# A two-block transformer on one NeuronCore: the first normalisation by column quarters, and four smaller moves in the first layer

## The chip, the core and the metric

The kernel is one program on one core of a Trainium2 chip. The metric is the device time of one launch in microseconds (us), median of the runs. The engines are TensorE (PE; its weight loads are listed as PEld), VectorE (DVE), ScalarE (ACT), GpSimd (POOL) and SyncE (SP), which here issues nearly all large DMAs. Each runs its own instructions in order, and they meet through semaphores.

## What is computed

A sequence of 256 tokens with model width 2048 goes through two layers of a first block (latent attention beside a gated convolution) and one layer of a second block. Only the first layer of the first block, and what feeds it, is touched:

```python
for l in range(2):
    mod = silu(c) @ ada_w[l] + ada_b[l]               # [2048] @ [2048, 6144]
    shift, scale, gate = split(mod, 3)
    h = rms_norm(x, norm_g[l]) * (1 + scale) + shift
    z = h @ w_in[l]
    q_lat, kv_lat, k_rope, mla_gate, conv_in, conv_gate = split(z)   # 512, 256, 64, 1024, 2048, 1024 columns
    q = rms_norm(q_lat) @ w_q_up[l];  kv = rms_norm(kv_lat) @ w_kv_up[l]
    # rms_norm and rotation of q and k, causal attention, times silu(mla_gate)
    u = (u_val + b) * sigmoid(u_gate + b)             # conv_in split in two
    u = silu(layer_norm(depthwise_conv31(u)))         # mean and variance over 1024 channels
    conv_out = (u @ w_pw[l] + b_pw[l]) * silu(conv_gate)
    x = x + gate * (concat(mla_out, conv_out) @ w_out[l])
```

## The kernel before

**Products.** Every large matrix product is a `Product`: blocks of 256 output columns, each of units of 4 row tiles (a unit of weights is 128 x 1024 floats, 0.5 MB). The activations are kept as `h_hi` + `h_lo` and each weight unit as `w_hi` (ACT rounds it) + `w_lo` (DVE subtracts, or POOL for the products `gate` and `cgate`), and PE adds three products per tile (L1705). A product with `lo=None` is native: no split, PE reads `w_raw`. There are 8 slots for raw units (`RAW`) and 4 for split ones (`PARTS`). SP, ACT, DVE and PE each walk the same list of products, written by hand in the order lat, krope, ua, ub, gate, cgate, kv, q, pw, outca, outcb, outm for a layer; `ahead` lets each engine prepare the next block beside the present one, and `beside` hooks put other work between units.

**The modulation vector.** `silu(c) @ ada_w` is made by loading `ada_w` in pieces of 128 x 1024 floats (0.5 MB) and adding each, scaled by a column of `c_act`, into an accumulator on DVE (L1137, in the first two groups L1156). A group of 32 pieces gives 2048 numbers; PE then sums it over the partitions (`reduce_mod`, L1729) and DVE adds the bias (`mod_out`, L1145). Groups 0 (shift) and 1 (scale) of layer 0 are loaded first of all through 8 slots; group 2 (gate) is spread by `ada=(...)` beside lat, krope and ua, group 3 beside ub, q and pw, group 4 beside outca and outcb. SP issues a piece right behind the weight unit it stands beside, and waits first for its slot of 4 (`ASLOTS`) to be consumed on DVE.

**The start.** SP loads the 64 pieces of groups 0 and 1 (L584), DVE adds them, PE transposes x, the small parameters and the convolution's taps (L1823, L1832, L1839), and sums the squares of x (L1737). After `mod_out(1)` DVE splits four weight units and makes the 16 tiles of h (L1216, L1221), and only then PE starts `lat`. After krope PE sums the squares of the latents (L1743).

**The convolution.** From the end of `ub`, DVE runs the 31 taps in four channel pairs (L1370, L1374), 2 steps beside each unit of `gate` and 6 beside each of `cgate`. Since POOL splits the weights of these two products, nothing else holds DVE there. `mod_out(2)` stands on DVE between the two products, `reduce_mod(2)` on PE ahead of `gate`. PE sums the conv output for the mean after units 2, 8 and 13 of `cgate` (`MEAN_STEPS`, L1872) and after unit 1 of `q` (`LAST_MEAN_STEP`), and its squares for the variance after unit 3 of `q` (`VAR_STEP`, L1718). Each sum waits for its pair's last tap. DVE subtracts the mean (L1389), ACT squares (L919), and after the variance DVE and ACT finish what `pw` reads.

## Time and profile before

| | us |
|---|---|
| median of 3 runs | 2280.22 (2279.74 to 2280.77) |
| profiled execution | 2277.91 |
| its span | 2276.1 |
| PE busy in it | 2148.8 (94%) |
| DVE busy in it | 1704.7 (75%) |
| ACT busy in it | 964.9 (42%) |

The page gives the busy time of each engine, 40 slices of the span, the chain that ended last and groups by line. The profiled execution is 1.8 us longer than its span and 2.3 us below the median. Matmuls overlap, so a row's duration is not its pace: the pace is the time from start to start.

### The profile page before, as it was taken

How to read it: one execution, taken by the hardware profiler on the slowest of the kernel's cores; microseconds unless marked ns; L12 is line 12 of the kernel's file. 1: busy time of each engine (PE TensorE's matmuls, PEld its weight loads, DVE VectorE, ACT ScalarE, POOL GpSimd, SP SyncE). 2: the span in 40 equal slices, each digit the busy share in tenths (PEclk: the TensorE clock that was granted, in tenths of full speed). 3: DMA queues.
4: the chain of work that ended last, by engine and by line, in shares of the span. 5: the costliest groups of instructions: out<-in, count | busy, mean ns of one | idle time of the engine just before them, and what ended most of it. 6: DMA issues, size and time to landing. Idle time of an engine off the chain costs nothing.

```text
span 2276.1 us, 39704 instructions
## 1 busy us (share of the span) xinstructions
PE 2148.8 (94%) x15541; PEld 2037.9 (90%) x15541; DVE 1704.7 (75%) x2347; ACT 964.9 (42%) x1512; POOL 214.3 (9%) x130
## 2 busy tenths in 40 slices
PE   2289999999999999999999999999999999999997
PEld 2289997889999978899999999999999999988886
DVE  6988997697999976877875887788876565653554
ACT  2144445325534353354454445455544444444443
POOL 0000481000006700033000000000000000000000
PEclk7599999999999999999999999999999999999999
DMA  9989965896898577969946996568866555566663
GB/s 329 351 286 360 300 175 192 275 324 222 296 373 256 149 268 252 316 177 293 364 135 224 375 372 199 173 201 272 275 207 207 180 181 184 184 214 186 191 193 122
DMA packets 390357, 559.41 MB, mean 246 GB/s; under 512 B 25544, under 2 KB 316944, under 8 KB 389725
## 3 DMA queue, kind: packets, MB, share of 16 engines
q1 hardware_dynamic: 386304, 550.70, 73.6%
q0 software_dynamic: 1456, 4.28, 0.8%
q10 hardware_dynamic: 2476, 2.82, 0.4%
q8 instruction: 76, 1.25, 0.2%
q14 instruction: 45, 0.36, 0.0%
HBM read 555.57 MB, written 2.18 MB: 245 GB/s over the span
## 4 chain that ended last, share of the span: by engine, by line
PE 85%; DVE 6%; ACT 3%; issue 3%; DMA 3%; SPq 0%; ACTq 0%; DVEq 0%
PE gemm L1705 80%; DMA ada_first<-in_ada_w 2%; DVE w_lo L1169 2%; DVE ada_even L1137 1%; PE stat L1729 1%; ACT w_hi L784 1%; DVE ada_acc L1156 0%; DVE scr L1216 0%; DVE ada_odd L1137 0%; PE bankT L1810 0%; DMA w_raw<-in_w_out 0%; PE gemm L1799 0%; PE bankO L1799 0%; PE stat L1872 0%; DVE h_lo L1221 0%
## 5 line engine op out<-in xcount | busy, mean ns | idle before, releaser
L1705 PE MATMUL gemm<-h_hi,w_hi 128*128 128x256 f32 (+1 forms) x3312 | 945.0, 285 | 17.6 <-DVE h_lo L1221 12.6
L1169 DVE TENSOR_TENSOR w_lo<-w_raw,w_hi 128x1024 fp32r<-128x1024 f32 x540 | 654.3, 1225 | 386.3 <-ACT w_hi L784 385.0
L1705 PE MATMUL gemm<-h_lo,w_hi 128*128 128x256 f32 (+1 forms) x3312 | 939.0, 284 | 0.0
L1705 PE MATMUL gemm<-h_hi,w_lo 128*128 128x256 f32 (+1 forms) x3312 | 939.0, 284 | 0.0
L784 ACT ACTIVATE w_hi<-w_raw 128x1024 fp32r<-128x1024 f32 (+1 forms) x604 | 619.7, 1041 | 694.6 <-PE gemm L1705 554.8
L1705 PEld LDWEIGHTS gemm<-h_hi,w_hi 128*128 128x128 f32 (+1 forms) x3312 | 634.5, 192 | 21.2 <-issue 15.9
L1705 PEld LDWEIGHTS gemm<-h_lo,w_hi 128*128 128x128 f32 (+1 forms) x3312 | 634.6, 192 | 0.6
L1705 PEld LDWEIGHTS gemm<-h_hi,w_lo 128*128 128x128 f32 (+1 forms) x3312 | 634.3, 192 | 0.3
L1137 DVE SCALAR_TENSOR_TENSOR ada_even<-ada_raw,c_act,ada_even 128x1024 f32<-128x1024 f32 x160 | 210.5, 1316 | 4.9 <-DMA ada_raw<-in_w_ada 1.7
L658 POOL TENSOR_TENSOR w_lo<-w_raw,w_hi 128x1024 fp32r<-128x1024 f32 x64 | 160.9, 2518 | 413.5 <-ACT w_hi L784 413.2
L1137 DVE SCALAR_TENSOR_TENSOR ada_odd<-ada_raw,c_act,ada_odd 128x1024 f32<-128x1024 f32 x128 | 169.5, 1325 | 5.3 <-DMA ada_raw<-in_ada_w 1.8
L1705 PE MATMUL gemm<-w_hi,G_hi 128*128 128x512 f32 x352 | 137.9, 392 | 1.8 <-DVE G_lo L1630 1.8
L1705 PE MATMUL gemm<-w_lo,G_hi 128*128 128x512 f32 x352 | 137.1, 389 | 0.0
L1705 PE MATMUL gemm<-w_hi,G_lo 128*128 128x512 f32 x352 | 137.0, 389 | 0.0
L1705 PE MATMUL gemm<-mixsrc,w_raw 128*128 128x256 f32 x512 | 115.3, 380 | 1.6 <-ACT krT L771 1.6
L1705 PEld LDWEIGHTS gemm<-mixsrc,w_raw 128*128 128x128 f32 x512 | 95.6, 190 | 14.2 <-ACT krT L771 2.2
L1374 DVE SCALAR_TENSOR_TENSOR bankT<-u_pad,dwT,bankT 128x256 f32<-128x256 f32 x232 | 91.2, 480 | 0.1
L1374 DVE SCALAR_TENSOR_TENSOR bankS<-u_pad,dwT,bankS 128x256 f32<-128x256 f32 x232 | 91.2, 480 | 0.0
L1705 PEld LDWEIGHTS gemm<-w_hi,G_hi 128*128 128x128 f32 x352 | 66.1, 188 | 15.3 <-DVE G_lo L1630 2.0
L1705 PEld LDWEIGHTS gemm<-w_lo,G_hi 128*128 128x128 f32 x352 | 66.1, 188 | 14.0
L1705 PEld LDWEIGHTS gemm<-w_hi,G_lo 128*128 128x128 f32 x352 | 66.1, 188 | 13.5
L1705 PE MATMUL gemm<-m_hi,w_hi 128*128 128x256 f32 x256 | 73.2, 286 | 2.5 <-DVE m_lo L1261 2.5
(350 smaller groups left out, 2661.1 us busy)
## 6 DMA issues: line engine op xcount, KB each, us to landing
w_raw<-in_w_in SPq DMA_DIRECT2D x264, 512.0 KB, 6.0
w_raw<-in_w_up SPq DMA_DIRECT2D x176, 512.0 KB, 3.5
ada_raw<-in_ada_w SPq DMA_DIRECT2D x160, 512.0 KB, 7.0
ada_raw<-in_w_ada SPq DMA_DIRECT2D x160, 512.0 KB, 6.4
w_raw<-in_w_out SPq DMA_DIRECT2D x96, 512.0 KB, 6.3
w_raw<-in_w_down SPq DMA_DIRECT2D x88, 512.0 KB, 3.7
ada_first<-in_ada_w SPq DMA_DIRECT2D x32, 512.0 KB, 8.8
ada_late<-in_w_ada SPq DMA_DIRECT2D x32, 512.0 KB, 5.2
```

The lines of the kernel that those rows point to most:

```text
L658: pool.tensor_tensor(w_lo[:, fixed % PARTS, 0:sz], w_raw[:, fixed % RAW, 0:sz], w_hi[:, fixed % PARTS, 0:sz].bitcast(F32), ALU.subtract).t ...
L784: act.activation(w_hi[:, fixed % PARTS, 0:sz], w_raw[:, fixed % RAW, 0:sz], ACT.Copy).then_inc(w_hi_done, 1)
L1137: dve.scalar_tensor_tensor(out=acc, in0=(ada_late if n == 11 else ada_raw)[:, slot, :], scalar=c_act[:, 0 if n < 6 else 1, bass.ds(m, 1)], ...
L1169: dve.tensor_tensor(w_lo[:, fixed % PARTS, 0:sz], w_raw[:, fixed % RAW, 0:sz], w_hi[:, fixed % PARTS, 0:sz].bitcast(F32), ALU.subtract).th ...
L1374: ins = dve.scalar_tensor_tensor(out=conv[:, ch, :] if k == TAPS - 1 else acc, in0=src, scalar=w, in1=acc, op0=ALU.mult, op1=ALU.add)
L1705: last = pe.matmul(half(g, k, q), left, right, start=(kt == 0 and j == 0 and (q == 0 or g.wide)), stop=(u == len(g.units) - 1 and t == nk ...
L1729: last = pe.matmul(stat[:, CB2 * t:CB2 * t + P], acc[:, j * AC + t * P:j * AC + (t + 1) * P], ones_and_halves[:, CB2:], start=(j == 0), st ...
```

## The change

**Start.** `FSLOTS` is 10, and groups 0 and 1 are loaded by column quarters: one piece now holds one row of every 16 of the matrix (`(k j)`, j = 16), and of it 512 columns of each of the two groups, so packets of 2 KB where they had 4 KB. Of the 16 pieces of a quarter, PE takes four itself (`BY_PE`, eight matmuls each with the piece as weights and `c16`, 16 columns, moving) and DVE adds the other twelve; `first_reduce` adds DVE's part in the same bank. `first_tiles` then makes 4 tiles of h. The products lat and krope of layer 0 become one product `first` of 4 blocks, which keeps all four in the `gemm` banks and adds 4 row tiles per quarter. SP loads its weights after the tenth piece of each quarter. The rope angles, the transposes of parameters and taps, and the small DMAs of ACT are spread over the quarters.

**Group 2** of layer 0 is added beside ua and ub (16 pieces each); `reduce_mod(2)` goes behind `gate` on PE in layer 0, while `mod_out(2)` keeps its place on DVE. **Groups 3 and 4** of layer 0 are placed by the table `SPREAD`. **The mean's last sum** goes to kv's unit 6, the **variance** to q's unit 1. **k's scaling** moves from DVE to ACT. **The latent sums** are made in two halves after units 4 and 5 of ua, in both layers, and their root and rows after units 8 and 13. ua and outm run as one body without a loop.

```diff
-FSLOTS = 8
+FSLOTS = 10
+W_AHEAD = 10
+ROPE_STEP = 5
+FROUNDS = -(-2 * AU // FSLOTS)
...
-LAST_MEAN_STEP = 1
-VAR_STEP = 3
+LAST_MEAN_STEP = 6
+VAR_STEP = 1
+LATENT_STEP, ROOT_STEP, ROWS_AT = 4, 8, 13
...
+QUARTERS = 4
+KQ = KT // QUARTERS
+FROWS = DM // P
+FCOLS = AC // 2
+BY_PE = (0, 1, 7, 11)
+PAR_EARLY = 10
+PAR_SPLIT = 24
+SUM_COLS = 16
+SPREAD = {"kv": [1] * 6 + [0] * 2, "q": [1] * 4 + [2] * 4, "pw": [1, 1, 1, 0] * 2, "outca": [2] * 8, "outcb": [2] * 8,
+          "outm": [0, 1] * 8}
 MOD_STEP = 1
 UP_FIRST = 8
...
+            if l == 0:
+                first = G["first"] = product("first", wi, QUARTERS, CB, full, QUARTERS, "a", h_hi, h_lo, plain(0))
...
+        pieces = [(n, j) for n in (3, 4) for j in range(AU)]
+        for name, counts in SPREAD.items():
+            g = G[name, 0]
+            g.ada, g.plan = None, []
+            for c in counts:
+                g.plan.append(pieces[:c])
+                pieces = pieces[c:]
...
+            def ada_load_first(qt, j):
+                m = FROWS * qt + j
+                slot = m % FSLOTS
+                if m >= FSLOTS:
+                    if by_pe(m - FSLOTS):
+                        sp.wait_ge(first_by_pe, pieces_up_to(m - FSLOTS, True))
+                    else:
+                        sp.wait_ge(ada_used, pieces_up_to(m - FSLOTS, False))
+                src = a["ada_w"][0][:, 0:2 * GROUP].rearrange("(k j) (g n) -> k j g n", j=FROWS, g=2)[
+                    :, j, :, FCOLS * qt:FCOLS * (qt + 1)]
+                sp.dma_start(first_slot(slot)[:, 0, :].rearrange("p (g n) -> p g n", g=2), src).then_inc(ada_loaded[slot], 16)
+            def load_first(qt):
+                for b, (k0, nk) in enumerate([(KQ * qt, KQ)] * 4):
+                    n, fixed = first.unit(0, qt, b)
+                    if fixed >= RAW:
+                        sp.wait_ge(w_used, n - RAW + 1)
+                    c, cols = first_cols(b)
+                    src = first.weights.rearrange("(k p) n -> p k n", p=P)[:, k0:k0 + nk, c:c + cols]
+                    dst = w_raw[:, fixed % RAW, 0:nk * cols].rearrange("p (k n) -> p k n", k=nk)
+                    sp.dma_start(dst, src).then_inc(w_loaded[fixed % RAW], 16)
...
+            for qt in range(QUARTERS):
+                for j in range(FROWS):
+                    if j == W_AHEAD:
+                        load_first(qt)
+                    ada_load_first(qt, j)
+            load(G["ua", 0], 0, 0)
...
+            def late_consts(part):
+                for x in (par_dmas[PAR_EARLY:PAR_SPLIT], par_dmas[PAR_SPLIT:])[part]:
+                    par_load(*x, const_loaded)
+                if part == 0:
+                    return
+                for l in range(LAYERS):
+                    act.dma_start(dw_rows[:, l, :], a["dw_w"][l]).then_inc(const_loaded, 16)
+                    for s, v in enumerate((a["q_norm_g"], a["k_norm_g"])):
...
+                act.wait_ge(k_inverse, l + 1)
+                act.wait_ge(k_rope_out, l + 1)
+                for t in range(TT):
+                    for h in range(NH):
+                        ins = act.activation(k_tok[:, t, h, :], k_tok[:, t, h, :], ACT.Copy,
+                                             scale=ss[:, 0, t * NH + h:t * NH + h + 1])
...
-                    link(dve.reciprocal(ss[:, 0, :], ss[:, 0, :]))
-                    dve.wait_ge(k_rope_out, l + 1)
-                    for t in range(TT):
-                        for h in range(NH):
-                            ins = dve.tensor_scalar(k_tok[:, t, h, :], k_tok[:, t, h, :],
-                                                    ss[:, 0, t * NH + h:t * NH + h + 1], None, ALU.mult)
-                    ins.then_inc(qk_ready, 1)
+                    dve.reciprocal(ss[:, 0, :], ss[:, 0, :]).then_inc(k_inverse, 1)
...
+            def first_tiles(qt):
+                first_low(qt, 0)
+                first_low(qt, 1)
+                cols = slice(KQ * qt, KQ * (qt + 1))
+                sums_ = first_sums(qt)[:, 0:2 * KQ * SUM_COLS].rearrange("p (g t c) -> p g t c", g=2, c=SUM_COLS)[:, :, :, 0]
+                bias_ = par[:, 0:2 * KT].rearrange("p (g t) -> p g t", g=2)[:, :, cols]
+                done, count = (first_taken, qt // 2 + 1) if qt % 2 == 0 else (stat_read, USE[f"first{qt}"] + 1)
+                if qt % 2 == 0:
+                    dve.wait_ge(first_summed, qt // 2 + 1)
+                else:
+                    stat_wait(dve, f"first{qt}")
+                dve.tensor_tensor(mod[:, 0:2, cols], sums_, bias_, ALU.add).then_inc(done, 1)
+                dve.wait_ge(done, count)
+                link(dve.scalar_tensor_tensor(out=gainA[:, cols], in0=mod[:, 1, cols], scalar=1.0,
+                                              in1=par[:, 3 * KT + KQ * qt:3 * KT + KQ * (qt + 1)], op0=ALU.add, op1=ALU.mult))
+                for t in range(KQ * qt, KQ * (qt + 1) + 2):
+                    if t < KQ * (qt + 1):
+                        dve.scalar_tensor_tensor(out=scr[:, t, :], in0=xT[:, t, :], scalar=gainA[:, t:t + 1],
+                                                 in1=rstd[:, 0, :], op0=ALU.mult, op1=ALU.mult).then_inc(t_ready, 1)
+                    if t >= KQ * qt + 2:
+                        c = t - 2
+                        dve.wait_ge(h_hi_ready, c + 1)
+                        dve.scalar_tensor_tensor(out=h_lo[:, c, :], in0=scr[:, c, :], scalar=mod[:, 0, c:c + 1],
+                                                 in1=h_hi[:, c, :].bitcast(F32), op0=ALU.add,
+                                                 op1=ALU.subtract).then_inc(h_ready, 1)
+                first_low(qt, 2)
+                first_low(qt, 3)
...
+            def first_piece(qt, j):
+                m = FROWS * qt + j
+                slot = m % FSLOTS
+                if j == BY_PE[0]:
+                    if qt % 2:
+                        stat_write(pe, f"first{qt}")
+                    elif qt:
+                        pe.wait_ge(first_taken, qt // 2)
+                pe.wait_ge(ada_loaded[slot], 16 * (m // FSLOTS + 1))
+                for t in range(2 * KQ):
+                    last = pe.matmul(first_sums(qt)[:, t * SUM_COLS:(t + 1) * SUM_COLS],
+                                     first_slot(slot)[:, 0, t * P:(t + 1) * P], c16[:, j, :],
+                                     start=(j == BY_PE[0] and t == 0), stop=False, skip_group_check=True)
+                last.then_inc(first_by_pe, 1)
...
+            def first_reduce(qt):
+                pe.wait_ge(ada_used, pieces_up_to(FROWS * (qt + 1) - 1, False) if qt < QUARTERS - 1 else 2 * AU)
+                for t in range(2 * KQ):
+                    last = pe.matmul(first_sums(qt)[:, t * SUM_COLS:(t + 1) * SUM_COLS],
+                                     first_acc[:, qt % 2, t * P:(t + 1) * P], ones[:, 0:SUM_COLS],
+                                     start=False, stop=(t == 2 * KQ - 1), skip_group_check=True)
+                last.then_inc((first_summed, stat_ready)[qt % 2], 1)
...
+            for qt in range(QUARTERS):
+                more = BY_PE if qt + 1 < QUARTERS else ()
+                for j in more[0:2]:
+                    first_piece(qt + 1, j)
+                first_unit(qt, 0)
+                first_unit(qt, 1)
+                for j in more[2:3]:
+                    first_piece(qt + 1, j)
+                first_unit(qt, 2)
+                first_unit(qt, 3)
+                for j in more[3:]:
+                    first_piece(qt + 1, j)
+                if qt == 1:
+                    par_turned()
+                if more:
+                    first_reduce(qt + 1)
             pe.wait_ge(halves_done, 1)
-            reduce_mod(0)
...
+                def latent_sums(_, n, l=l):
+                    if n == LATENT_STEP:
+                        pe.wait_ge(lat_squared, l + 1)
+                        stat_write(pe, f"lat{l}")
+                    if n in (LATENT_STEP, LATENT_STEP + 1):
+                        for j in range(3 * (n - LATENT_STEP), 3 * (n - LATENT_STEP) + 3):
+                            last = token_sums(0 if j < 4 else TT, lat_sq[:, j, :], j == 0, j in (3, 5))
+                        if n == LATENT_STEP + 1:
+                            last.then_inc(stat_ready, 1)
+                    if n == ROWS_AT:
+                        inverse_rows(f"lat{l}", 2)
...
-                reduce_mod(3 * l + 2)
+                if l:
+                    reduce_mod(3 * l + 2)
                 multiply(G["gate", l])
+                if not l:
+                    reduce_mod(3 * l + 2)
...
-                multiply(G["kv", l])
+                multiply(G["kv", l], lambda _, n: mean(CT // 2 - 1) if n == LAST_MEAN_STEP else None)
                 def variance(_, n):
-                    if n == LAST_MEAN_STEP:```

What stands in a row on each engine at three places. First DVE between `ub` and the mean's subtraction in layer 0 (bankS and bankT hold the taps' running sums; L1370/L1591 open a pair). Before:

```order
L1370 TENSOR_SCALAR bankT<-u_pad,dwT,par 128x256 x2
L1145 TENSOR_TENSOR mod<-stat,par 128x16
L1374 SCALAR_TENSOR_TENSOR bankT<-u_pad,dwT,bankT 128x256 x58
L1374 SCALAR_TENSOR_TENSOR conv<-u_pad,dwT,bankT 128x256 x2
L1370 TENSOR_SCALAR bankS<-u_pad,dwT,par 128x256 x2
```

and, after the change, from the same read of `stat` on:

```order
L1309 TENSOR_TENSOR mod<-stat,par 128x16
L1595 SCALAR_TENSOR_TENSOR bankT<-u_pad,dwT,bankT 128x256 x58
L1595 SCALAR_TENSOR_TENSOR conv<-u_pad,dwT,bankT 128x256 x2
L1591 TENSOR_SCALAR bankS<-u_pad,dwT,par 128x256 x2
L1595 SCALAR_TENSOR_TENSOR bankS<-u_pad,dwT,bankS 128x256 x58
L1595 SCALAR_TENSOR_TENSOR conv<-u_pad,dwT,bankS 128x256 x2
L1591 TENSOR_SCALAR bankT<-u_pad,dwT,par 128x256 x2
L1595 SCALAR_TENSOR_TENSOR bankT<-u_pad,dwT,bankT 128x256 x58
L1595 SCALAR_TENSOR_TENSOR conv<-u_pad,dwT,bankT 128x256 x2
L1293 MEMSET ada_odd 128x1024
L1301 SCALAR_TENSOR_TENSOR ada_odd<-ada_raw,c_act,ada_odd 128x1024 x6
L1610 SCALAR_TENSOR_TENSOR conv<-stat,conv 128x2048
```

The read of `stat` stands in the same place, inside the second pair, but what fills `stat` now comes behind `gate` on PE; and a memset and six pieces stand between the last tap and the mean's subtraction.

Second, SP's queue at `kv` (the weights of kv, two blocks, then a piece behind each block), after the change:

```order
L691 DMA w_raw<-in_w_in 128x4x256 x28
L691 DMA w_raw<-in_w_kv_up 128x2x256 x2
L678 DMA ada_raw<-in_ada_w 128x1x1024
L691 DMA w_raw<-in_w_kv_up 128x2x256
L678 DMA ada_raw<-in_ada_w 128x1x1024
L691 DMA w_raw<-in_w_kv_up 128x2x256
L678 DMA ada_raw<-in_ada_w 128x1x1024
```

Before, no piece stood beside kv. Third, DVE at the start of the third quarter after the change (c_102 is `c16`):

```order
L1335 TENSOR_TENSOR w_lo<-w_raw,w_hi 128x1024 x2
L1350 TENSOR_TENSOR mod<-bankO,par 128x2x4
L1352 SCALAR_TENSOR_TENSOR gainA<-mod,par 128x4
L1356 SCALAR_TENSOR_TENSOR scr<-xT,gainA,rstd 128x256 x3
L1361 SCALAR_TENSOR_TENSOR h_lo<-scr,mod,h_hi 128x256
L1356 SCALAR_TENSOR_TENSOR scr<-xT,gainA,rstd 128x256
L1361 SCALAR_TENSOR_TENSOR h_lo<-scr,mod,h_hi 128x256 x3
L1335 TENSOR_TENSOR w_lo<-w_raw,w_hi 128x1024
L1335 TENSOR_TENSOR w_lo<-w_raw,w_hi 128x256
```

Before, one such stretch of 16 tiles stood behind all 64 pieces.

## Rows read from the trace of the kernel before

**Rows 1.** The page: busy time of each engine.

```profile
PE 2148.8 (94%) x15541; PEld 2037.9 (90%) x15541; DVE 1704.7 (75%) x2347; ACT 964.9 (42%) x1512; POOL 214.3 (9%) x130
```

**Rows 2.** Waits of PE: what, for what, us in total, times, longest.

```profile
PE stat L1729 <- DVE mod L1145: 39.3, 1, 39.3
PE bankS L1823 <- ACT xT L771: 19.7, 1, 19.7
```

**Rows 3.** Chain that ended last, 60 to 170 us: start, us, what.

```profile
109.29 1.28 DVE ada_acc L1156
110.81 5.19 PE stat L1729 x32
...
116.30 4.63 DVE w_lo L1169 x4
121.05 1.28 DVE scr L1216 x3
...
122.87 42.20 PE gemm L1705 x336
165.07 2.57 PE stat L1743 x24
```

**Rows 4.** Windows: PE, PEld, DVE, ACT, POOL busy; clock, DMA share, GB/s.

```profile
8.00:36.00 28.00, 2.79 (x12) 2.42 (x12) 18.21 (x15) 0.00 (x0) 0.00 (x0) 0.74 1.03 395
...
140.00:164.00 24.00, 24.00 (x204) 24.00 (x203) 20.09 (x21) 9.86 (x15) 0.00 (x0) 1.00 1.05 358
168.00:172.00 4.00, 4.00 (x23) 4.00 (x23) 4.00 (x4) 3.91 (x7) 0.00 (x0) 0.57 1.08 376
...
386.00:426.00 40.00, 39.24 (x165) 30.92 (x165) 32.26 (x49) 15.30 (x52) 0.00 (x0) 1.00 1.04 364
```

**Rows 5.** The same of PE alone: PE busy, clock, DMA share, GB/s.

```profile
124.00:128.00 4.00, 4.00 (x23) 0.58 0.14 52
```

**Rows 6.** Timeline of PE in the start: start, us, line, operation.

```profile
59.28 7.03 PE L1839 MATMUL bankT<-ident,dw_rows 31*128 31x31 f32 x32
```

**Rows 7.** Critical chain, 255 to 400 us, in layer 0 from ub's end on.

```profile
262.73 1.79 PE stat L1729 x16
264.52 54.71 PE gemm L1705 x456
...
353.50 24.73 PE gemm L1705 x128
...
379.12 2.30 DVE conv L1389
...
381.45 1.91 ACT ln_sq L919
...
387.98 10.59 PE gemm L1705 x32
...
399.05 1.10 PE gemm L1705 x4
```

**Rows 8.** Timeline of DVE in the convolution and behind it.

```profile
292.34 0.17 DVE L1145 TENSOR_TENSOR mod<-stat,par 128x16 f32<-128x16 f32 x1
...
340.46 0.98 DVE L1370 TENSOR_SCALAR bankT<-u_pad,dwT,par 128x256 f32<-128x256 f32 x2
...
364.08 0.86 DVE L1374 SCALAR_TENSOR_TENSOR conv<-u_pad,dwT,bankT 128x256 f32<-128x256 f32 x2
...
400.27 3.76 DVE L1422 TENSOR_SCALAR k_tok<-k_tok,ss 128x192 f32<-128x192 f32 x16
```

**Rows 9.** Timeline of PE at kv's end and in q.

```profile
359.09 19.13 PE L1705 MATMUL gemm<-w_raw,lat 128*128 128x256 f32 x80
...
378.92 5.32 PE L1705 MATMUL gemm<-w_raw,lat 128*128 128x384 f32 x16
384.08 3.62 PE L1718 MATMUL stat<-ln_sq,ones_and_halves 128*128 128x256 f32 x16
```

**Rows 10.** Issues of DMA by line: KB each, median us to landing.

```profile
w_raw<-in_w_kv_up SPq DMA_DIRECT2D x16, 256.0 KB, 2.8
```

410 lines of the change are left out of this document (268 added, 142 removed).

## Prediction

> **What bounds the kernel now.** I read the page first: PE is busy for 2148.8 of 2276.1 us [rows 1], so 127 us are left. The waits of PE name two long ones, both ahead of the first large product: 39.3 us for the second modulation vector and 19.7 us for the copy of x [rows 2]. Behind the start, only PE's own work, or a wait that is put in its way, can move the end. The chain then dates the start: DVE ends the last of 64 pieces at 110.6, PE sums them to 116.0, four weight units are split to 120.9, PE begins at 122.87 and ends lat and krope at 165.07 [rows 3]. In that stretch DMA is the supplier: 395 GB/s with 4 KB packets alone, and 358 GB/s where 1 KB weight packets are mixed in [rows 4]. Last I read layer 0 from 262 to 400 on both engines, since the diff moves a sum there. On PE one product follows the other [rows 7, 9]. DVE ends the taps at 364.9 [rows 8], 13 us ahead of the sum behind the kv row (359.09 + 19.13 = 378.2) that needs the last of them [rows 9].
>
> **Start.** Behind 165.07 the same products follow as now, so the gain is 165.07 less the time at which PE ends `first`.
>
> Bytes ahead of it: 64 pieces of 0.524 MB are 33.5, the latent weights 2048 x 832 x 4 B are 6.8, x is 2.1, small ones 0.5: 43 MB. At 395 GB/s for all that is 109 us, at 358 it is 120 us [rows 4]. Packets of 2 KB lie between the two kinds that the rows show, so I take 115, plus 2 for the beginning. DVE's work in a quarter is 12 pieces of 1.28, three and a quarter splits of 1.2 and eight tile operations of 0.43 [rows 3]: 23 us, against 27 to 29 us of DMA, so it follows. But at each border DVE frees no slot for some 8 us, and I add 4 us in all. The last piece lands at 121.
>
> Behind it: DVE adds it (1.3), PE sums (16 records, at 5.19/32 = 0.16 each: 2.6), bias and gain 0.4, three scr and one h_lo 1.7 [rows 3]. Then 84 matmuls. At the low level, 1.2 GHz, 256 columns take 0.213; at the high one the row of 456 shows 0.12 [rows 7]. The first 24 low are 5.1 and 60 high 7.2. The splits lie beside PE's sum. Together 18.3, so `first` ends at 139 to 140. I take 140: **25 us gained**. Bounds: all bytes at 395 and no loss at the borders, 132 (33 gained); all at 358 and 8 us lost there, 150 (15 gained).
>
> PE's added work is 16 pieces of 16 records (2.6 each). It is hidden as long as PE's quarter is shorter than that of DMA: 10.4 + 2.6 + 84 matmuls (10.1 to 17.9) = 23 to 31 us, against 27 to 29. The taps' transposes (7.0 [rows 6]) stand in the second quarter, in what PE has left; if they had no cover, they would cost 7 there.
>
> **Latent sums.** They are loads of weights with one column moving. Behind the 24 of them in layer 0 the clock is granted at 0.57, which is mostly the 1.2 GHz level, from 168 to 172, and 23 matmuls fit in 4 us where 4/0.12 = 33 would [rows 4]: 10 x 0.12 = 1.2 us, and some ahead of it. In two halves between units PE's dense work resumes sooner. I take **1.5 us gained**, bounds 0 and 3 (both layers).
>
> **Late gate sum.** On PE it costs 1.79 in either place. But DVE reads it and stays where it was. In the times of the trace before, DVE reaches that read at 292.3 and finds it done [rows 8]. Now PE does gate first: 384 matmuls of 0.12 from 262.7 end at 308.8, the sum at 310.6 [rows 7]. DVE waits from 292.3 to 310.8, **18.3 us**, with all later taps queued behind, since it is in order. A pair takes 24.4 (340.5 to 364.9), so pairs 1 to 3 end at 334.4, 358.8 and 383.2 instead of 316.1, 340.5 and 364.9 [rows 8].
>
> PE asks for pair 2 at 352.6 (0.87 ahead of the 353.50 row [rows 7]) and gets it at 358.8: **6.2 us lost**; the sum ends at 359.7, two units of cgate (5.8) at 365.5. The kv row of 19.13 holds 80 records, 64 of kv and 16 of q; two units of q are 5.32, so a kv unit is 13.8/8 = 1.7 [rows 9]. Six of them end at 375.8.
>
> **Pieces by plan.** The fifth piece beside kv needs the slot of the first, which DVE adds behind the last tap: 383.2 + memset 0.9 (an estimate) + 1.3 = 385.4. Behind that piece in SP's queue stand the weights of kv's block 6. They go out at 386.2 and land after 2.8 [rows 10] plus 1.4 for the piece ahead: 390.4. So PE waits there **14.6 us**, and this covers the wait for the last tap. Block 6 ends at 392.1, the mean's last sum at 393.0.
>
> **Mean and variance sooner.** DVE has by then added its six pieces (384.1 + 7.7 = 391.8), subtracts in 2.3: 395.3; ACT squares in 1.9: 397.3 [rows 7]. PE does the last kv unit and two of q (1.7 + 5.3) to 400.0: no wait. Variance 3.6, six units of q at 2.65 15.9 [rows 9]: 419.5. What pw reads is ready before: it took 11.4 us from the variance's end at 387.7 [rows 9] to 399.05 [rows 7], and PE has 15.9 of q here. So pw starts at 419.5 against 399.05: **20.4 us lost** in layer 0. Of that the wait of 0.48 ahead of pw goes in both layers (387.98 + 10.59 = 398.57 [rows 7]): 1 us gained. Bounds of the loss: 22 at the top; 13 if SP's queue does not bind and only the taps do (6.2, then 383.2 - 377.4 = 5.8 at the mean, and 1 at the variance).
>
> **The rest at nothing.** k's scaling, 3.8 us on DVE [rows 8], becomes 16 ACT instructions. ACT is busy for 15.3 of the 40 us there [rows 4]; without that cover PE would wait up to 8 (16 of 0.5) ahead of the transposes. Eight pieces moved into outm: DVE has a block of 5.8 us of PE's and needs 2.4 + 1.3 + 1.2 = 4.9; uncovered they would be 10. Beside ua and ub each unit still has one piece, 1.05 MB in 2.88 us. Layer 1 keeps its sum ahead of gate, so it has no such stall. Bounds 0 to 4 lost.
>
> **Sum.** Span: -25 - 1.5 + 20.4 - 1 = -7.1. Profiled execution 2277.9 - 7.1 = 2270.8; the median stood 2.3 above it: **2273 us**.
>
> **Two rules of the Trainium skill.** The page "DMA: Bandwidth & Descriptors" (Bandwidth) gives about 358 GB/s as a core's share of HBM when both cores of a pair stream. The trace shows 395 with one core running [rows 4]. By that rule the 43 MB would take 120 us and the total would be 5 us more.
>
> "TensorE: Matmul & The Clock Gate" (HAM oscillation) says that an array which waits for data between bursts drops to its slow clock and begins every burst there. The trace agrees for the first burst: 0.58 from 124 to 128 [rows 5]. What that would do to the quarters is rival 2.
>
> **Rivals.**
> 1. *DVE's wait costs PE next to nothing* (the convolution catches up, or the read comes later than I think). For it: 13 us of lead. Against: the wait is 18.3, and a later pair has 24.4 us on DVE against at most 18.1 between two sums on PE. Then the start counts, and 1.5 us at kv's block 6 (365.8 + 1.3 + 0.8 + 4.2 = 372 against 369.5 to 370.5 for PE): -25 - 1.5 - 1 + 1.5 = -26: 2254. Chance 0.17.
> 2. *PE bounds the quarters at the low clock* (the other side). The place is each quarter; the price is its 84 matmuls at 0.213 instead of 0.12. Then a quarter is 31 us, the first sum comes at 44, and with the taps (7) `first` ends at 44 + 3 x 31 + 7 + 21 = 165: nothing gained, and with 20.4 lost the time is 2298. The sign turns against the change by more than 4.6 us when `first` ends behind 152. For it: 0.58 in the first burst [rows 5]. Against: dense matmuls follow each other for 10 us and more in each quarter, and 23 in those 4 us are already more than the 19 of an all-low stretch. Chance 0.08.
> 3. *The parameters land late* and hold PE in its second quarter, and with it the slots. The copies of x waited 19.7 us for ACT [rows 2], which issues these DMAs. A hold of 8 us beyond the slack: 2281. Chance 0.12.
> 4. *The start streams at 395 GB/s*: `first` ends at 133, 2266. Chance 0.13.
>
> The forecast has 0.50.
>
> **How the numbers follow.** A measurement of this kernel can tell 0.2%, 4.6 us, from no change. Faster by more is below 2275.7: rivals 1 and 4, and 0.40 of the forecast's 0.50: 0.70. Within it: 0.10 of the forecast and most of rival 3: 0.21. Slower: rival 2 and the rest: 0.09. The range goes from rival 1 (2253) to where rival 2 decides (2284).
>
> **What would show it.** In the profile after: `first` ends near 140; DVE waits some 18 us for the sum of group 2, at about 266; PE waits near 326 for the conv output and near 349 for kv's weights; pw starts near 393, although ua starts 25 us earlier; the clock is full behind the latent sums. If DVE's wait is there and PE's are not, rival 1 holds. If `first` ends behind 150 with PE busy at a low clock, rival 2.

## The result and the profile after

The changed kernel takes 2290.13 us (median of 5, 2288.06 to 2291.11), the kernel before 2279.92 on the same chip: a ratio of 1.0038 (95% interval 1.0027 to 1.005). It is 10.2 us slower, where the forecast was 7 faster, and the time lies outside the range. The profiled execution took 2289.61 with a span of 2287.8, 11.7 above the 2276.1 of before.

PE's busy time went up by 52 us [rows 1]; that alone says nothing yet, since most of it is the start, where PE used to wait:

```profile
PE 2201.2 (96%) x15798; PEld 2089.3 (91%) x15798; DVE 1673.0 (73%) x2302; ACT 976.3 (43%) x1543; POOL 214.1 (9%) x130
```

PE's waits (what, for what, us in total, times, longest). The two of [rows 2] are gone. The first and the last row are new and lie in layer 0, the other two are the new start:

```profile
PE gemm L1920 <- DMA w_raw<-in_w_kv_up: 12.3, 1, 12.3
PE stat L2072 <- DVE first_acc L1324: 9.1, 1, 9.1
PE bankO L2045 <- DMA ada_raw<-in_ada_w: 8.8, 1, 8.8
PE stat L2172 <- DVE conv L1595: 6.3, 1, 6.3
```

The chain that ended last, in the start (start, us, what), which answers to [rows 3]:

```profile
36.15 8.80 PE stat L1952 x32
...
59.59 15.78 DMA ada_raw<-in_ada_w
...
76.74 3.60 PE stat L2072 x16
80.34 6.83 PE bankO L2045 x32
87.17 7.54 PE gemm L2090 x48
94.70 1.69 PE bankO L2045 x16
...
103.26 5.93 PE bankT L2110 x32
109.19 3.53 PE bankO L2072 x16
112.72 6.83 PE stat L2045 x32
...
135.54 1.80 PE stat L2072 x16
...
139.59 12.81 PE gemm L2090 x84
```

L2045 is a piece that PE adds, L2072 the sum that closes a quarter, L2090 `first`, L2110 the taps' transposes. Read it backwards: `first` ends at 139.59 + 12.81 = **152.40**, not at 140. The last link is as long as I said (16.9 us from 135.54 on, against 18.3 less the 1.3 of DVE's last piece). But the last sum begins at 135.5, where I had the last piece landed at 121. From 76.74 to 135.54 the chain is PE alone, but for 0.4 us of a copy on ACT at 102.8: 58.8 us for two quarters. And 76.74 is late already: it hangs on a transfer of 15.8 us, which SP could issue only when DVE had freed its slot at 59.6.

Windows of the start (PE, PEld, DVE, ACT, POOL busy; clock, DMA share, GB/s), answering to [rows 4]:

```profile
30.00:45.00 15.00, 12.44 (x51) 11.10 (x52) 6.42 (x5) 0.39 (x2) 0.00 (x0) 0.68 1.05 382
45.00:60.00 15.00, 13.55 (x98) 13.47 (x97) 14.00 (x22) 5.41 (x9) 0.00 (x0) 0.77 1.07 358
60.00:75.00 15.00, 7.69 (x67) 7.59 (x67) 11.04 (x18) 3.49 (x4) 0.00 (x0) 0.85 0.85 289
75.00:90.00 15.00, 13.26 (x62) 13.26 (x63) 12.80 (x19) 3.50 (x7) 0.00 (x0) 0.50 0.92 292
105.00:120.00 15.00, 15.00 (x71) 14.94 (x72) 9.04 (x16) 5.54 (x9) 0.00 (x0) 0.50 1.03 351
```

My 115 us were 43 MB at 374 GB/s. From 30 to 60 us the rows come near that (382, 358), from 60 to 90 they show 290. SP's own waits say what it lacked: slots. Of its first 140 us it waited 21.2 for pieces that DVE adds (the first row and 2.9 more in another) and 16.6 for pieces that PE adds (the second row and 5.8 more); from 55 to 80 us it was 15.4, all for DVE's:

```profile
SPq L661 <- DVE first_acc L1324: 18.3, 19, 3.7
SPq L661 <- PE bankO L2045: 10.8, 4, 4.1
```

The kernel before had such dips too, with rows of 4 KB, which [rows 4] leave out (columns as above):

```profile
40.00:50.00 10.00, 8.87 (x41) 7.51 (x40) 5.32 (x5) 8.09 (x20) 0.00 (x0) 0.90 0.82 272
60.00:70.00 10.00, 10.00 (x50) 9.94 (x50) 9.54 (x19) 2.27 (x4) 0.00 (x0) 0.54 1.00 377
70.00:80.00 10.00, 1.52 (x14) 1.33 (x12) 9.55 (x8) 0.00 (x0) 0.00 (x0) 0.81 0.54 175
```

From 105 to 120 PE is busy for all of it at a clock of 0.50 in the changed kernel: there the 16 records of a piece take 3.4 us (6.83/2), at the full clock 1.69.

Layer 0, timelines of DVE and of PE (in brackets the wait ahead and what ended it), answering to [rows 7 to 9]:

```profile
297.05 0.17 DVE L1309 TENSOR_TENSOR mod<-stat,par 128x16 f32<-128x16 f32 x1 [18.17 <-PE stat L1944]
```

```profile
345.31 2.07 PE L2172 MATMUL stat<-conv,ones_and_halves 128*128 128x256 f32 x4 [6.26 <-DVE conv L1595]
377.15 3.75 PE L1920 MATMUL gemm<-w_raw,lat 128*128 128x256 f32 x8 [12.35 <-DMA w_raw<-in_w_kv_up]
...
407.52 7.72 PE L1920 MATMUL gemm<-conv,w_raw 128*128 128x256 f32 x35
```

DVE waits 18.2 for the sum of group 2 (forecast 18.3), PE 6.3 for the second pair (6.2) and 12.3 for kv's weights (14.6). pw starts 255.1 us behind the end of `first`; before it was 399.05 - 165.07 = 234.0 [rows 3, 7].

The span's 11.7 us, landmark by landmark in the two chains (in the one after, ub ends within a longer row, at 202.89 + 46.07 = 248.96, with 384 matmuls of 0.12):

| stretch | before | after | difference |
|---|---|---|---|
| start to the end of `first` (lat, krope) | 165.07 | 152.40 | -12.7 |
| to the end of ub | 97.66 | 96.56 | -1.1 |
| gate to outca's begin | 173.25 | 196.27 | +23.0 |
| outca, outcb | 79.50 | 79.42 | -0.1 |
| outm to the first product of layer 1 | 49.95 | 52.07 | +2.1 |
| layer 1 to its gate sum | 137.54 | 137.53 | 0 |
| layer 1, gate sum to the copies of q and k | 164.65 | 163.39 | -1.3 |
| the rest | 1408.48 | 1410.16 | +1.7 |

### The profile page after: what moved, and what is told of

Its sections match the earlier page's. It is cut to its first block, busy times and chain, and to the rows that moved or that the text cites. A ratio compares the mean times of both kernels' runs of the same rounds, so it can differ in the third digit from the quotient of the medians.

```text
span 2287.8 us, 40078 instructions
## 1 busy us (share of the span) xinstructions
PE 2201.2 (96%) x15798; PEld 2089.3 (91%) x15798; DVE 1673.0 (73%) x2302; ACT 976.3 (43%) x1543; POOL 214.1 (9%) x130
## 4 chain that ended last, share of the span: by engine, by line
PE 85%; DVE 8%; ACT 3%; issue 2%; DMA 1%; ACTq 0%; SPq 0%; DVEq 0%
PE gemm L1920 76%; DVE bankT L1595 2%; PE gemm L2090 2%; DMA ada_raw<-in_ada_w 1%; DVE bankS L1595 1%; PE bankO L2045 1%; DVE w_lo L1377 1%; DVE ada_even L1301 1%; ACT w_hi L890 1%; DVE ada_odd L1301 1%; PE stat L1944 1%; PE stat L2045 0%; PE bankT L2029 0%; DVE scr L1426 0%; PE stat L1952 0%
## 5 line engine op out<-in xcount | busy, mean ns | idle before, releaser
L1920 PE MATMUL gemm<-h_hi,w_hi 128*128 128x256 f32 (+2 forms) x3200 | 912.7, 285 | 11.4 <-DVE h_lo L1431 5.7
L1377 DVE TENSOR_TENSOR w_lo<-w_raw,w_hi 128x1024 fp32r<-128x1024 f32 (+1 forms) x524 | 638.1, 1231 | 377.1 <-ACT w_hi L890 376.0
L1920 PE MATMUL gemm<-h_lo,w_hi 128*128 128x256 f32 (+2 forms) x3200 | 907.2, 283 | 0.0
L1920 PE MATMUL gemm<-h_hi,w_lo 128*128 128x256 f32 (+2 forms) x3200 | 907.0, 283 | 0.0
L890 ACT ACTIVATE w_hi<-w_raw 128x1024 fp32r<-128x1024 f32 (+1 forms) x588 | 607.6, 1046 | 675.8 <-PE gemm L1920 580.9
L1920 PEld LDWEIGHTS gemm<-h_hi,w_hi 128*128 128x128 f32 (+2 forms) x3200 | 613.7, 192 | 14.7 <-issue 9.6
L1920 PEld LDWEIGHTS gemm<-h_lo,w_hi 128*128 128x128 f32 (+2 forms) x3200 | 613.7, 192 | 0.6
L1920 PEld LDWEIGHTS gemm<-h_hi,w_lo 128*128 128x128 f32 (+2 forms) x3200 | 613.6, 192 | 0.3
L1301 DVE SCALAR_TENSOR_TENSOR ada_even<-ada_raw,c_act,ada_even 128x1024 f32<-128x1024 f32 x160 | 214.6, 1341 | 8.6 <-DMA ada_raw<-in_w_ada 5.5
L1301 DVE SCALAR_TENSOR_TENSOR ada_odd<-ada_raw,c_act,ada_odd 128x1024 f32<-128x1024 f32 x128 | 163.8, 1280 | 14.0 <-DMA ada_raw<-in_ada_w 10.4
L1920 PE MATMUL gemm<-w_hi,G_hi 128*128 128x512 f32 x352 | 137.8, 392 | 1.8 <-DVE G_lo L1845 1.8
L1920 PE MATMUL gemm<-w_lo,G_hi 128*128 128x512 f32 x352 | 137.1, 389 | 0.0
L1920 PE MATMUL gemm<-w_hi,G_lo 128*128 128x512 f32 x352 | 137.0, 389 | 0.0
L1920 PE MATMUL gemm<-mixsrc,w_raw 128*128 128x256 f32 x512 | 115.3, 380 | 1.6 <-ACT krT L875 1.6
L1920 PEld LDWEIGHTS gemm<-mixsrc,w_raw 128*128 128x128 f32 x512 | 95.6, 190 | 14.2 <-ACT krT L875 2.2
L1595 DVE SCALAR_TENSOR_TENSOR bankT<-u_pad,dwT,bankT 128x256 f32<-128x256 f32 x232 | 91.3, 491 | 0.1
L1595 DVE SCALAR_TENSOR_TENSOR bankS<-u_pad,dwT,bankS 128x256 f32<-128x256 f32 x232 | 91.2, 486 | 0.0
L1920 PE MATMUL gemm<-w_raw,lat 128*128 128x256 f32 (+1 forms) x256 | 71.9, 441 | 12.3 <-DMA w_raw<-in_w_kv_up 12.3
L1920 PEld LDWEIGHTS gemm<-w_hi,G_hi 128*128 128x128 f32 x352 | 66.1, 188 | 15.4 <-DVE G_lo L1845 2.0
L1920 PEld LDWEIGHTS gemm<-w_raw,lat 128*128 128x128 f32 x256 | 49.4, 194 | 32.4 <-issue 12.7
L1920 PEld LDWEIGHTS gemm<-w_lo,G_hi 128*128 128x128 f32 x352 | 66.1, 188 | 13.9
```

Of the source, the lines that this page charges most:

```text
L890: act.activation(w_hi[:, fixed % PARTS, 0:sz], w_raw[:, fixed % RAW, 0:sz], ACT.Copy).then_inc(w_hi_done, 1)
L1301: dve.scalar_tensor_tensor(out=acc, in0=(ada_late if n == 11 else ada_raw)[:, slot, :], scalar=c_act[:, 0 if n < 6 else 1, bass.ds(m, 1)], ...
L1377: dve.tensor_tensor(w_lo[:, fixed % PARTS, 0:sz], w_raw[:, fixed % RAW, 0:sz], w_hi[:, fixed % PARTS, 0:sz].bitcast(F32), ALU.subtract).th ...
L1595: ins = dve.scalar_tensor_tensor(out=conv[:, ch, :] if k == TAPS - 1 else acc, in0=src, scalar=w, in1=acc, op0=ALU.mult, op1=ALU.add)
L1920: last = pe.matmul(half(g, k, q), left, right, start=(kt == 0 and j == 0 and (q == 0 or g.wide)), stop=(u == len(g.units) - 1 and t == nk ...
```

## Experiments

Ratios and differences are against runs of the kernel before on the same chip; on it the changed kernel stands at +10.2 us. "End of `first`" is read in the chain of each. The changed kernel and four kernels with the same start (e1, e3, g8, g7) ended it at 152.40, 152.19, 152.02, 152.48 and 154.86, so that a difference under 2.8 us shows nothing there. Each of these ends is read from one profiled execution.

**e1_early_sum.** The late sum undone.

```diff
-                if l:
-                    reduce_mod(3 * l + 2)
+                reduce_mod(3 * l + 2)
                 multiply(G["gate", l])
-                if not l:
-                    reduce_mod(3 * l + 2)
```

> The changed kernel with one part undone: in layer 0 TensorE sums the modulation vector of group 2 ahead of gate again. Theory A (the whole loss in layer 0 hangs on VectorE's wait of 18.2 us for that sum, and the waits of 6.3 and 12.3 us on TensorE follow from it): all three waits go, the time falls by 18 to 21 us from 2290.1 to about 2270. Theory B (the six pieces beside kv hold SyncE's queue by themselves, whatever VectorE does): the wait for kv's weights stays at 5 us or more, and the time is 2275 or more.

Measured: 2272.31 against 2281.77, ratio 0.9965 (0.995 to 0.9979), 9.5 us under the kernel before. The waits for the conv output and for kv's weights are both gone from the list of waits. So one line of PE's order costs 19.7 us (10.2 + 9.5; by the intervals give or take 4, and 17.3 between the two spans), and with it put back the rest of the change is a gain. Theory A. But the early place isn't free either. In e1's chain:

```profile
248.93 3.50 issue
252.44 3.76 PE stat L1944 x16
```

PE stands for 3.5 us ahead of the sum. The profile names nothing that it waits for, but the sum needs all pieces of group 2, and DVE ends the last of them, beside ub, at 252.3. The sum then takes 3.76 us and not 1.80. The kernel before had no such wait, since its group 2 was added by the end of ua. All variants with the early sum have these 3.5 us, so their gains below are net of some 5.

**g8_read_moved.** The sum stays late, but DVE reads it later.

```diff
-                mod_out(3 * l + 2)
-                through(G["cgate", l], none, lambda _, v: convolve(...))
+                if l:
+                    mod_out(3 * l + 2)
+                def convolve_and_read(_, v, l=l):
+                    if not l and v == 4:
+                        mod_out(3 * l + 2)
+                    convolve(range(split + 6 * v, min(split + 6 * v + 6, conv_steps)))
+                through(G["cgate", l], none, convolve_and_read)
```

> The changed kernel with the sum of group 2 behind gate, as it is there, but VectorE reads it 24 steps of the taps later, beside cgate. Theory A (the loss in layer 0 is only that VectorE, which works in order, stands at the read; the place of the sum on TensorE costs nothing): VectorE waits less than 1 us, the waits of 6.3 and 12.3 us on TensorE go, and the time is that of e1_early_sum, about 9.5 us under the kernel before. Theory B (the late sum itself hurts TensorE or the pieces' slots): the time is less than 6 under the kernel before.

Measured: 2270.23 against 2281.45, ratio 0.9949 (0.9932 to 0.9965), 11.2 us under. DVE's timeline has no wait at the read (no bracket):

```profile
297.68 0.17 DVE L1309 TENSOR_TENSOR mod<-stat,par 128x16 f32<-128x16 f32 x1
```

So a late sum does no harm; a read left where it was does. One remnant: kv's weights still come 3.6 us late. This version pays that where e1 pays the 3.5 us ahead of the sum; it was not joined with the better starts below.

**e2_before_late.** The kernel before with the late sum alone.

> The kernel before with one part of the change alone: the sum of group 2 in layer 0 behind gate. Theory A (the late sum is bad only together with the pieces beside kv and with the mean's last sum moved ahead into kv): VectorE waits 18 us, TensorE waits 6.2 us for the second pair of taps, and nothing more, because the last sum of the mean stands in q; 2279.9 + 6.2 = 2286. Theory B (the late sum alone costs what the change loses in layer 0): 2300.

Measured: 2291.07 against 2281.77, ratio 1.0039 (1.0025 to 1.0053): +9.3, neither 6.2 nor 20. The wait is 6.3 as expected and there is no second one. What was missing is what stands behind the wait, in the chain (and in windows, columns as above):

```profile
360.32 2.07 PE stat L1875 x4
362.40 25.88 PE gemm L1705 x128
```

```profile
358.00:362.00 4.00, 1.68 (x5) 1.41 (x5) 4.00 (x11) 0.00 (x0) 0.00 (x0) 0.51 0.00 0
362.00:366.00 4.00, 4.00 (x23) 3.91 (x23) 4.00 (x11) 0.00 (x0) 0.00 (x0) 0.64 0.01 2
366.00:370.00 4.00, 4.00 (x32) 3.90 (x31) 4.00 (x11) 0.66 (x2) 0.00 (x0) 1.00 0.21 66
```

The four records that take 0.87 at the full clock take 2.07, and PE comes back to full clock some 5 us later. The next 128 records take 25.88, and 24.73 in the kernel before [rows 7]. A wait of 6.3 us thus costs 1.2 and 1.15 more, 8.6 in all, and that is what ub's end to outca's begin grew by in the two chains.

**e3_kv_free.** `SPREAD` with kv `[0] * 8`, q `[2] * 8`, pw `[1] * 8`.

> The changed kernel, but no modulation piece is read beside kv: q has two beside each unit and pw one (the number is the same, 64). Theory A (the wait of 12.3 us for kv's weights is SyncE's in-order queue, where a piece that wants its slot stands ahead of them): that wait goes; in its place TensorE waits 3 to 5 us for the last tap, so that 7 to 9 us come back and the time is about 2282. Theory B (the same stall returns at q, where the fifth piece now waits for its slot): less than 4 us come back, 2287 or more.

Measured: 2284.08 against 2281.77, ratio 1.0018 (1.0008 to 1.0027): 7.9 us of the 10.2 come back. The wait for kv's weights is gone, and PE waits for the last tap instead:

```profile
344.93 2.08 PE L2172 MATMUL stat<-conv,ones_and_halves 128*128 128x256 f32 x4 [6.27 <-DVE conv L1595]
369.32 1.62 PE L2172 MATMUL stat<-conv,ones_and_halves 128*128 128x256 f32 x4 [3.41 <-DVE conv L1595]
```

Theory A: the 12.3 us were SP's in-order queue, with 3.4 of the taps hidden beneath them.

**e4_two_pieces.** `BY_PE = (0, 1)`: the first of five kernels on the start.

> The changed kernel, but in each quarter TensorE adds two of the 16 pieces of weights and not four; VectorE adds 14. Theory A (behind 80 us TensorE is what bounds the first product: it is busy without a gap from 80 to 135): the four pieces of 1.7 us there, and one or two in the first quarters, go from its path, the first product ends 7 to 12 us ahead of 152.4, and the time is about 2281. Theory B (the transfers bound the start, at 245 to 385 GB/s, and TensorE only follows): the first product ends within 2 us of 152.4, and the time stays at 2290. Theory C (VectorE becomes the bound with 28 more us of pieces... that is 2.6 us more in each quarter): it ends later, and the time is above 2292.

Measured: 2290.64 against 2281.77, ratio 1.0045 (1.0028 to 1.0062); `first` ends at 152.0. Nothing is gained although PE has 8 pieces less. Its chain now runs over DVE from 107 on: DVE adds 14 pieces of 1.39 there, and its tile work of the third quarter begins late, at `w_lo`. The changed kernel has that delay too; DVE's waits from 60 to 140 us in it:

```profile
DVE w_lo L1335 <- ACT w_hi L997: 7.0, 1, 7.0
```

ACT's `w_hi` of the third quarter stands behind its copies of the parameters, and these wait for the 5.9 us of transposes on PE. So PE's and DVE's queues are equally long here, and one of them shortened gives nothing.

**g5_norm_sums_first** (e1, and the norm's column sums ahead of PE's third and fourth piece).

> The changed kernel with the sum of group 2 ahead of gate again (as in e1_early_sum, which was 9.5 us under the kernel before), and in the first quarter TensorE makes the 16 column sums of the norm ahead of its third and fourth piece instead of behind them. Theory A (the order of TensorE in the first quarter costs the start: the fourth piece lands at 32.5 us, and 8.8 us of sums, rstd and all tile work of the first quarter stand behind it, so that slots come free late): the tile work of the first quarter begins 5 to 9 us sooner, the transfers of quarter two go on sooner, and the first product ends 3 to 7 us sooner; the time is 13 to 16 us under the kernel before. Theory B (the slots' turnover later binds again, or TensorE behind 80 us): the first product ends within 2 us of 152.4, and the time stays about 9.5 under the kernel before.

Measured: 2273.9 against 2281.45, ratio 0.9963 (0.995 to 0.9975); `first` ends at 153.50. Theory B: the first quarter's tile work comes sooner, but the second quarter's sum waits for its last pieces until 77.7, as before.

**h10_4kb_rows** (e1, and each piece read as 1024 neighbouring columns; these are other columns, so the modulation vector is another).

```diff
-                src = a["ada_w"][0][:, 0:2 * GROUP].rearrange("(k j) (g n) -> k j g n", j=FROWS, g=2)[
-                    :, j, :, FCOLS * qt:FCOLS * (qt + 1)]
+                src = a["ada_w"][0][:, AC * qt:AC * (qt + 1)].rearrange("(k j) n -> k j n", j=FROWS)[:, j, :]
...
```

> As e1_early_sum, but every piece of the first two groups is read as 1024 neighbouring columns (one stretch of 4 KB a row) and not as two times 512 (2 KB); the bytes are the same, and the columns are other ones than the computation wants, so its result is another. Theory A (2 KB stretches slow the stream): the start runs at up to 395 GB/s, the last piece of the second quarter lands at 66 to 70 us and not at 75, and the first product ends 5 us or more ahead of 152.4. Theory B (the stream is slow for another reason: the small packets beside it, or slots that come free late): the second quarter's last piece lands within 2 us of 75, and the first product ends within 2 us of 152.4.

Measured: 2268.21 against 2281.14, ratio 0.9946 (0.993 to 0.9963). Chain and windows:

```profile
71.84 3.60 PE stat L2071 x16
...
130.41 1.80 PE stat L2071 x16
...
134.45 12.68 PE gemm L2089 x84
```

```profile
30.00:45.00 15.00, 13.63 (x66) 12.42 (x66) 7.47 (x6) 2.92 (x4) 0.00 (x0) 0.75 1.03 401
60.00:75.00 15.00, 9.04 (x67) 8.94 (x66) 13.21 (x14) 3.37 (x4) 0.00 (x0) 0.78 0.99 359
```

The second quarter's sum begins 5.1 us sooner than in e1 (76.89), `first` ends at 147.1, 5.1 sooner. The same bytes in rows of 4 KB run at 401 and 359 GB/s, where the changed kernel has 382 and 289 (e1 382 and 294). Behind it the stretch to the last sum is the same: 130.41 - 71.84 = 58.6.

**h12_more_bytes** (e1 and five transfers of 0.524 MB more in quarters two and three).

> As e1_early_sum, but SyncE issues five transfers more of 0.524 MB each (2.6 MB) in the second and third quarter, into a tile that is not in use then; nobody computes with them. Theory A (the transfers bound the start, at 335 to 360 GB/s): the first product ends 7 to 8 us later than in e1_early_sum, and the time is 2 us or less under the kernel before. Theory B (TensorE or VectorE bounds it and the queue has slack): it ends less than 3 us later, and the time is 7 or more under the kernel before.

Measured: 2283.9 against 2281.14, ratio 1.0015 (1.0005 to 1.0025), 2.8 over the kernel before and 12 over e1, more than theory A asked. Chain:

```profile
86.65 3.59 PE stat L2085 x16
...
145.52 1.80 PE stat L2085 x16
```

`first` ends at 162.4. The second sum is 9.8 us later than in e1, with only 1.6 MB of the 2.6 ahead of it (4.7 us at 335 GB/s). But the edit does more than add bytes: SP waits for the norm's sums ahead of the first added transfer, for 13.2 us, and the stream falls to 266 GB/s from 30 to 45 us, where e1 has 382. So this run doesn't tell what bytes alone cost. From the second sum on it is again 58.9, though two more transfers lie in that stretch. Together with h10 it says: up to 77 us the start hangs on when the pieces land, and behind it on PE's queue.

**h9_taps_sooner** (e1, with parameters and taps turned at the end of PE's first quarter).

```diff
-                if qt == 1:
+                if qt == 0:
                     par_turned()
```

> As e1_early_sum (9.5 us under the kernel before), but TensorE turns the parameters and the taps at the end of its first quarter, in front of the sum for the second, where it waits 9 us for VectorE, and ScalarE copies them behind the four w_hi of its second quarter. Theory A (behind 80 us TensorE's own work bounds the start, and with it ScalarE's w_hi of the third quarter, which stand behind these copies): the first product ends 5 to 8 us ahead of 152.4 and the time is 15 to 17 us under the kernel before. Theory B (the transfers bound it: three kernels with less work on one engine or the other ended the first product between 150.7 and 154.8): it ends within 3 us of 152.4, and the time is 8 to 12 us under the kernel before.

Measured: 2276.41 against 2281.14, ratio 0.9977 (0.9967 to 0.9986); `first` ends at 156.2, neither theory. The longest of PE's waits in the start is now

```profile
PE bankT L2104 <- DMA g_qk<-in_k_norm_g: 9.5, 1, 9.5
```

The last constants, which ACT issues at 52 to 57 us behind the first quarter's tiles, land at 77.4, some 20 us later, behind the pieces of SP. This is rival 3's mechanism, hidden in the changed kernel by the transposes' place.

**i1_constants_sooner** (h9, and ACT issues these constants right behind the others, ahead of its wait for the norm).

```diff
                     late_consts(0)
+                    late_consts(1)
...
-                if qt == 0:
-                    late_consts(1)
```

> As h9_taps_sooner (sum of group 2 ahead of gate; parameters and taps turned at the end of TensorE's first quarter), but ScalarE issues the last constants ahead of its wait for the norm, at about 29 us and not at 52: there they landed at 77.4 us, and TensorE waited 9.5 us for them. Theory A (from 77 us on TensorE's queue bounds the start: in four kernels it took 58.6 to 58.9 us from the end of the second sum's wait to the last sum's end, whatever the transfers did): without the taps this stretch is 7 us or more shorter and the first product ends 144 to 148; 16 to 19 us under the kernel before. Theory B (the last transfers land at 131 or so in any order): the first product ends at 150 to 152, and the time is 9 to 12 us under the kernel before.

Measured: 2269.21 against 2281.26, ratio 0.9954 (0.9939 to 0.9969), 12.1 under the kernel before; `first` ends at 146.2. Chain:

```profile
72.53 6.20 PE bankT L2110 x32
78.74 3.53 PE stat L2072 x16
...
104.85 1.80 PE bankO L2072 x16
...
116.80 8.81 DMA ada_raw<-in_ada_w
...
134.15 12.06 PE gemm L2090 x84
```

The transposes now lie beside transfers. From the second sum to the end of `first` it is 67.5 us, where the changed kernel has 75.7 (152.40 - 76.74), and the chain of the last quarter runs over a transfer again. The profile bears theory A out (146.2 lies in its 144 to 148), the time only in part: 12.1 under and not 16 to 19, 2.6 better than e1, with intervals that overlap. The profiled execution, 2265.8, was the fastest of four (up to 2273.2), so its 146.2 may flatter the version.

**i2_and_two_pieces** (i1 with `BY_PE = (0, 1)`).

> As i1_constants_sooner, and TensorE adds two of 16 pieces and not four. TensorE's quarter is then about 3.5 + 6.8 + 12.7 = 23 us, VectorE's 14 pieces of 1.39 and 10 of tile work = 29. Theory A (TensorE alone binds): it ends sooner than i1 by 2 to 3 us. Theory B (VectorE, or the transfers at 350 GB/s with their last piece at about 131, bind next): it ends no sooner than i1, or up to 5 us later.

Measured: 2270.8 against 2281.26, ratio 0.9953 (0.9938 to 0.9968); `first` ends at 151.1, 4.9 later than i1. Theory B: all of the last two quarters' chain is DVE's 14 pieces and tiles. Four pieces on PE were right.

**g6_64_columns and i3_mended.** c16 with 64 equal columns instead of 16; i3 is i1 with that and with g7's `SPREAD`.

> As e1_early_sum, but each matmul by which TensorE adds a piece of modulation weights, or sums VectorE's part, moves 64 equal columns and not 16 (the sum that is read is the same). Theory A (TensorE's clock is granted at the low level in the quarters because these matmuls move little): the clock stays at 2.4 GHz from 80 to 135 us, a record takes 0.107 us there and not 0.213, the first product ends 5 to 10 us ahead of 152.4, and the time is 14 to 20 us under the kernel before. Theory B (the clock falls for the waits, not for the columns): the records at 1.2 GHz stay, the first product ends within 2 us of 152.4, and the time is 8 to 11 us under the kernel before. Theory C (64 columns cost TensorE time by themselves): the first product ends later.

> As i1_constants_sooner, with 64 columns moved by the matmuls of the pieces and with outm's pieces beside its first eight units. If theory A of i1 holds, 17 to 20 us under the kernel before; if theory B holds, 11 to 13.

Measured: g6 2270.03 against 2281.45, ratio 0.995 (0.9935 to 0.9965), `first` ends at 150.7, 1.5 sooner than e1, which is inside the spread. i3 2269.56 against 2281.26, ratio 0.9946 (0.9933 to 0.996), `first` ends at 148.5. The clock does answer to the columns, in i3 (first row) against i1 (second):

```profile
110.00:120.00 10.00, 10.00 (x87) 10.00 (x87) 9.37 (x11) 2.14 (x3) 0.00 (x0) 1.00 1.09 363
```

```profile
110.00:120.00 10.00, 10.00 (x56) 10.00 (x56) 9.37 (x10) 1.06 (x1) 0.00 (x0) 0.61 1.08 362
```

But where the clock is low already it stays so with 64 columns too: the 32 records behind the wait for the second sum are at 0.213 (6.83 from 80.85 on in g6), and from 105 to 120 us, behind the taps' transposes, g6 had 0.50 like e1. And what PE gains it waits away for DVE and the transfers: it was 4.4 busy of 10 us from 120 to 130 in i3. Of the two theories on g6, B holds for the time.

**g7_outm_early** (e1 with outm's pieces `[1] * 8 + [0] * 8`).

> As e1_early_sum, but the eight pieces beside outm stand beside its first eight units, not beside every second. Theory A (the 2.1 us that the way from outm's beginning to the first product of layer 1 has become longer, 49.95 to 52.07, is VectorE's work on the last piece and splits in front of the squares of the norm): these 2.1 us come back, and the time is about 11.5 us under the kernel before. Theory B (it is the new order of the squares, outm's blocks being one body of eight now): it stays at 52.1, and the time is 9.5 under the kernel before.

Measured: 2271.78 against 2281.45, ratio 0.9954 (0.9938 to 0.9971), indistinguishable from e1. Outm to the first product of layer 1 takes 51.2 us, between the 50.0 of before and 52.1. In the changed kernel the chain into the norm holds a split and a piece, ahead of the norm's square on DVE:

```profile
566.16 1.22 DVE w_lo L1377
567.38 1.19 DVE ada_even L1301
```

In g7 this is gone, but outm waits for weights instead (`w_raw<-in_w_out` enters the chain). At most half of the 2.1 us is thus explained. Not run: the latent sums all at once in the changed kernel; their 1.1 us is read from the traces only. **h11_together** (e1 with h9's and g6's edits, without the earlier constants) gave 2276.48 against 2281.14, ratio 0.9979 (0.997 to 0.9989): the late constants of h9 again, with a wait of 10.6 us.

So every version with the early sum or the moved read, but h12 with its added bytes, beat the kernel before. The lowest ratio of a whole computation is i3's, 0.9946; those of e1, g6, g7, g8, i1 and i2 overlap it.

## Why the prediction was wrong

**What bounds the kernel** was right: the time moved by the start and by the waits put in PE's way, and by little else.

**Start: the step that failed.** 25 us were forecast and 12.7 came; this is 12.3 of the 18.8 us between forecast (-7.1) and span (+11.7). Its tail was right (16.9 us against 17). The sum that should begin at 122.3 began at 135.5. Two steps failed, and the trace dates them:
- *The stream up to the second quarter's end: some 10 us.* I put rows of 2 KB between the 358 and the 395 GB/s of [rows 4], took 374, and gave 4 us to the borders. By these terms the second quarter's last piece (22.8 MB in order) lands at about 65; it landed at 75.4. With the same bytes in rows of 4 KB the sum behind it comes 5 us sooner (h10). The rest was not taken apart. What the trace shows of it are SP's waits for slots, 37.8 us in the first 140 (not all of it lost, since other pieces are on their way meanwhile), where my sum had 4 us in all, and the dips of the kernel before (272 and 175 GB/s), which I had not read.
- *The overlap of PE's queue: 2 to 3 us.* From the second sum to the last my terms gave the transfers 56 us (twice 27, and the borders). PE took 58.8, and 58.0 to 58.9 in e1, e3, g5, g7, g8, h10 and h12, which keep this order of PE. The quarters themselves were priced right: 25.7 and 26.4 us, where I had 23 to 31, and the four pieces of one are 6.83 + 1.69 + 1.69 = 10.2 us, where I had 10.4. What had no cover is the turning of parameters and taps, 6.8 us from 102.4 on: PE had nothing left there, having begun this quarter at 76.7. One sum sooner, PE stands idle for 9 us, but there they would have waited for the constants (h9); with these issued sooner too (i1), `first` ends 6 us ahead of e1.

So PE's queue set the end behind 77 us, but what made `first` late was mostly lost before. Rival 2 named the sign, "if `first` ends behind 150 with PE busy at a low clock", and its turning point, 152, was hit at 152.4. Its mechanism was another: its quarter was 31 us, with all 84 matmuls at the low clock, and the measured ones took 12 to 13 us and not 17.9. I gave it 0.08 and argued from the dense matmuls of each quarter alone. The window of before from 60 to 70 us, above, would have warned me: 10.00 of 10.00 us busy at 0.54, on the transposes of [rows 6] (7.03 us for 32) and what stands around them.

The forecast cited the Trainium skill's "DMA: Bandwidth & Descriptors" (Bandwidth) for 358 GB/s. Its sum, 5 us more, would have been nearer, but not by its reason: here one core alone read 401 GB/s over 15 us (h10), and part of the low stretches went with the row size.

**Latent sums.** 1.1 us in layer 0 (forecast 1.5 for both), nothing in layer 1.

**Late gate sum and kv's pieces.** The mechanism was right in each link, and e1, g8 and e3 show them one by one: the read, the second pair, SP's queue. Its size was 23.0 against 20.4. (The sum took 0.5 too much off it: 399.05 stands behind layer 0's wait ahead of pw, so that wait was in the 20.4 already.) The term missing is the clock behind a wait, 2.35 us for 6.3 in e2. In the changed kernel it is seen twice: 2.07 for four records at 345.31, which costs nothing more, since PE waits for kv's weights afterwards anyway, and 3.75 for eight at 377.15, where kv's pace is 1.7 for eight: 2.0 us. Another 0.8 lies behind pw, where PE waits for the copies of q. And PE's sum does not cost 1.79 "in either place": with group 2 beside ub the early place costs 3.5 us of waiting and 2.0 of clock (e1), which the prediction did not see as the late place's merit. Rival 1, that DVE's wait costs PE nothing, is dead: its 13 us of lead were less than 18.

**k's scaling and pw's wait**: with the variance sooner layer 1 gained 1.3 (forecast 0.5). **The rest at nothing** was 3.7: 2.1 into the norm of layer 1, and 1.6 in layer 2 (below).

## What to carry to other kernels

When a producer is moved later on one engine, move its reader on the in-order engine too, or cost everything queued behind the read; here one line cost 19.7 us, and with the reader moved the same late place was 11.2 us under the kernel before. A wait on TensorE costs more than its length. When a supply-bound stage is spread over more engines, ask for each buffer who frees it and when, and read the stream's rate over the whole stage and not in its best stretch. Then add up every engine's queue for the stage, with the small things that stand in it: two queues of equal length hide each other from any test that shortens only one.
